# Two attention memories stored with features on partitions, one array of parameters, and the first stage reordered

## The reference

```python
def _rmsnorm(x, g):
    y = xf * lax.rsqrt(jnp.mean(xf * xf, axis=-1, keepdims=True) + EPS)
    return (y * g.astype(jnp.float32)).astype(x.dtype)
...
h = _rmsnorm(x, g_mix[l])
sb_q, ..., xa_q, gate_pre = jnp.split(h @ w_in[l], offsets, axis=-1)
...
# cross attention of the first block: keys and values
k, v = jnp.split(_rmsnorm(mem, g_mem[l]) @ w_mem_kv[l], 2, axis=-1)
# each later layer L: keys and values from the raw second memory
mem_2 @ w_mem_k_2[L],  mem_2 @ w_mem_v_2[L]
```

## Time and profile before

| | |
|---|---|
| median of 3 runs | 1054.83 us (1052.07 to 1055.42) |
| the profiled execution | 1052.53 us, its span 1050.7 us |
| TensorE matmul busy | 1030.6 us, 98% of the span |
| VectorE, ScalarE busy | 730.9 us (70%), 654.1 us (62%) |
| DMA | 167.52 MB, mean 159 GB/s |
| mean granted TensorE clock | 0.997 of full |

### The profile page before, as it was taken

How to read it: one execution, slowest core, us unless ns; L and a number is a source line. 1 busy time by engine, 2 the same in 40 slices (tenths; PEclk the granted TensorE clock), 3 DMA queues, 4 the chain that set the end, 5 groups by cost and what they waited for, 6 DMA issues and landing times.

```text
span 1050.7 us, 19082 instructions
## 1 busy us (share of the span) xinstructions
PE 1030.6 (98%) x8048; PEld 922.0 (88%) x8048; DVE 730.9 (70%) x1085; ACT 654.1 (62%) x924; POOL 13.3 (1%) x18
## 2 busy tenths in 40 slices
PE   6999999999999999999999999999999999999996
PEld 5798987888989999988999998888799999988875
DVE  4684688885747788765565758977884656599686
ACT  6776576564456656544466678657755667776583
POOL 1000000000000000000000000100000000001000
PEclk9999999999999999999999999999999999999999
DMA  8663434666547655566544533422565455344231
GB/s 307 225 202 120 142 124 137 200 200 201 173 149 228 195 179 167 193 223 187 173 160 130 165 125 120 141 83 102 180 199 168 130 161 161 101 143 142 79 116 47
DMA packets 97831, 167.52 MB, mean 159 GB/s; under 512 B 7048, under 2 KB 32530, under 8 KB 97490
## 3 DMA queue, kind: packets, MB, share of 16 engines
q1 hardware_dynamic: 95776, 159.24, 47.3%
q0 software_dynamic: 1472, 5.51, 1.5%
q10 hardware_dynamic: 498, 1.55, 0.4%
HBM read 165.23 MB, written 1.05 MB: 158 GB/s over the span
## 4 chain that ended last, share of the span: by engine, by line
PE 95%; DVE 3%; DMA 1%; ACT 1%; issue 1%; SPq 0%; DVEq 0%
PE proj L598 13%; PE proj L589 13%; PE proj L600 13%; PE proj L599 13%; PE proj L591 13%; PE proj L590 13%; PE mix L935 1%; PE mix L979 1%; PE mix L936 1%; PE mix L634 1%; PE mix L659 1%; PE mix L642 1%; PE mix L968 1%; DVE wlo L1538 1%; DMA raw<-in_w_mem_kv 1%; PE mix L875 1%
## 5 line engine op out<-in xcount | busy, mean ns | idle before, releaser
L1538 DVE TENSOR_TENSOR wlo<-raw,whi 128x1024 fp32r<-128x1024 f32 (+3 forms) x303 | 355.4, 1202 | 139.9 <-ACT whi L1065 138.0
L1065 ACT ACTIVATE whi<-raw 128x1024 fp32r<-128x1024 f32 (+3 forms) x303 | 306.2, 1040 | 148.1 <-PE proj L600 66.5
L589 PE MATMUL proj<-act_hi,whi 128*128 128x256 f32 x1064 | 303.5, 285 | 0.6 <-ACT arena L1082 0.4
L591 PE MATMUL proj<-act_hi,wlo 128*128 128x256 f32 x1064 | 300.9, 283 | 0.0
L590 PE MATMUL proj<-act_lo,whi 128*128 128x256 f32 x1064 | 300.9, 283 | 0.0
L589 PEld LDWEIGHTS proj<-act_hi,whi 128*128 128x128 f32 x1064 | 203.1, 191 | 3.3 <-ACT arena L1082 1.2
L590 PEld LDWEIGHTS proj<-act_lo,whi 128*128 128x128 f32 x1064 | 203.2, 191 | 0.9
L591 PEld LDWEIGHTS proj<-act_hi,wlo 128*128 128x128 f32 x1064 | 203.2, 191 | 0.2
L598 PE MATMUL proj<-whi,y_hi 128*128 128x512 f32 (+1 forms) x340 | 135.1, 397 | 3.8 <-DVE wlo L1538 3.5
L599 PE MATMUL proj<-wlo,y_hi 128*128 128x512 f32 (+1 forms) x340 | 132.4, 389 | 0.0
L600 PE MATMUL proj<-whi,y_lo 128*128 128x512 f32 (+1 forms) x340 | 132.3, 389 | 0.0
(11 more groups left out here) (360 smaller groups left out, 1239.7 us busy)
## 6 DMA issues: line engine op xcount, KB each, us to landing
raw<-in_w_in SPq DMA_DIRECT2D x144, 512.0 KB, 4.4
raw<-in_w_up SPq DMA_DIRECT2D x88, 256.0 KB, 4.2
raw<-in_w_out SPq DMA_DIRECT2D x32, 512.0 KB, 4.3
raw<-in_w_down SPq DMA_DIRECT2D x22, 512.0 KB, 5.4
raw<-in_w_mem_kv SPq DMA_DIRECT2D x8, 512.0 KB, 9.1
raw<-in_w_mem_k SPq DMA_DIRECT2D x8, 512.0 KB, 4.0
raw<-in_w_o SPq DMA_DIRECT2D x8, 512.0 KB, 3.7
raw<-in_w_mem_v SPq DMA_DIRECT2D x8, 512.0 KB, 3.9
```

Source lines behind the costliest of these rows:

```text
L589: mm(o, wh[:, i, wc], hi[:, k0 + i, :], start=begin and j % 2 == 0, stop=False, skip_group_check=True)
L591: last = mm(o, wl[:, i, wc], hi[:, k0 + i, :], start=False, stop=end, skip_group_check=True)
L1065: fn(whi[c % SPLIT][:, 0:w], raw[c % SLOTS][:, 0:w], ACT.Copy).then_inc(s.w_hi, 1)
L1538: tt(wlo[c % SPLIT][:, 0:w], raw[c % SLOTS][:, 0:w], f32(whi[c % SPLIT][:, 0:w]), ALU.subtract).then_inc(s.w_lo, 1)
```

## The change

- Both memories are handed over with features on partitions (`[P, KT, SEQ]`). The first memory's tiles are rounded from SBUF, with no transposes (`mem_upper`, `mem_lower`). SP requests its halves ahead of pieces 0 and 2.
- All parameter rows become one array `params` of 128 x 284 float32, requested by ScalarE in one transfer; the 3 + 11 transposes and the copies of parameters out of PSUM go.
- The sums of squares of the memory now need a sum over partitions: ScalarE squares the whole memory, VectorE adds the eight tiles in one reduction with an inner stride of 256 elements, and TensorE adds over partitions by two matmuls with a column of ones.
- The scaled `x` is turned after half of xav (pieces 4 and 5) rather than before it. `x` is requested ahead of piece 5, not piece 4.
- The rest of the constants is requested after ScalarE has moved xav out; the `tree` table once 16 lower halves are made. The small instructions for lower bounds and rotary angles move behind the softmax of the cross attention, amid sbv.
- The second memory's two turns become one copy on ScalarE and one subtraction on VectorE each.

```diff
-STAGES1, STAGES2 = 8, 5
+STAGES1, STAGES2 = 6, 5
...
+    for name in ("mem", "mem_2"):
+        arrays[name] = np.ascontiguousarray(named[name][0].T.reshape(KT, P, SEQ).transpose(1, 0, 2))
...
-        MEM = ar(4096, NB, DM)
+        MEM, MEM_SQ, MEM_SUM = ar(14336, KT, SEQ), ar(4096, KT, SEQ), ar(8192, SEQ)
...
         def _(sp):
-            sp.dma_start(const[:, 0:P], a["const"][:, 0:P]).then_inc(s.ident_in, 16)
-            for b in range(NB):
-                sp.dma_start(MEM[:, b, :], a["mem"][0, b * P:(b + 1) * P]).then_inc(s.mem_in, 16)
             for c, loads in enumerate(pieces):
-                if c == SLOTS:
+                if c in (0, 2):
+                    half = slice(c * KT // 4, c * KT // 4 + KT // 2)
+                    sp.dma_start(MEM[:, half, :], a["mem"][:, half, :]).then_inc(s.mem_rest if c else s.mem_in, 16)
+                if c == SLOTS + 1:
                     sp.dma_start(X[:, :, :], a["x"][0].rearrange("(b p) d -> p b d", p=P)).then_inc(s.x_in, 16)
...
         def _(pool):
-            pool.wait_ge(s.x_in, 16)
+            pool.wait_ge(s.w_lo, 4 * SLOTS)
             pool.dma_start(TREE_IN[:, :], a["tree"]).then_inc(s.tree_in, 16)
...
# TensorE
+            project("xak", None, MEM_hi, MEM_lo, ready=lambda k: pe.wait_ge(s.mem_lo, k))
+            pe.wait_ge(s.mem_sum, 1)
+            for b in range(NB):
+                last = mm(mix[:, 3, 4 * b:4 * b + 4], MEM_SUM[:, b * P:(b + 1) * P], ONE4, start=True, stop=True)
+            last.then_inc(s.mem_ss, 1)
+            project("xav", None, MEM_hi, MEM_lo, part=(0, 2))
+            pe.wait_ge(s.norm_x, 1)
             pe.wait_ge(s.ident_in, 16)
-            pe.wait_ge(s.gains_in, 16 * 3)
-            for v in range(3):
-                last = nc.tensor.transpose(mix[:, 0, v * 8:(v + 1) * 8], STG8[:, v * P:(v + 1) * P], ident[0:8, 0:8])
-            last.then_inc(s.par_t, 1)
+            turn(KT, lambda k, b: XN[:, b, k * P:(k + 1) * P])
+            project("xav", None, MEM_hi, MEM_lo, part=(2, 4))
             pe.wait_ge(*stage(1, None))
-            pe.wait_ge(s.mem_in, 32)
-            turn(KT, lambda k, b: MEM[:, b, k * P:(k + 1) * P])
-            project("xak", None, MEM_hi, MEM_lo, ready=lambda k: pe.wait_ge(s.mem_lo, k))
...
             project("xaq", None, act_hi, act_lo)
...
-            turn(KT, lambda k, b: MEM2_AT[None][:, b, k * P:(k + 1) * P])
...
-                if L + 1 < LAYERS:
-                    pe.wait_ge(s.mem2_in, 16 * L + 32)
-                    turn(KT, lambda k, b: MEM2_AT[L][:, b, k * P:(k + 1) * P])
                 project("hgf0", L, act_hi, act_lo)
-                if L + 1 < LAYERS:
-                    pe.wait_ge(s.mem2_ok, L + 2)
...
# ScalarE
+            act.dma_start(par[:, :], a["params"]).then_inc(s.params, 16)
+            act.dma_start(const[:, 0:P], a["const"][:, 0:P]).then_inc(s.ident_in, 16)
...
+            mem_upper(range(KT // 2))
             split_until(2)
+            act.wait_ge(s.mem_rest, 16)
+            mem_upper(range(KT // 2, KT))
+            split_until(SLOTS)
+            fn(MEM_SQ, MEM, ACT.Square).then_inc(s.mem_sq, 1)
+            split_until(SLOTS + 1)
+            act.wait_ge(s.x_in, 16)
             for b in range(NB):
-                last = fn(XN[:, b, :], MEM[:, b, :], ACT.Square, accum_out=FIRST_SS[:, b:b + 1])
+                last = fn(XN[:, b, :], X[:, b, :], ACT.Square, accum_out=FIRST_SS[:, b:b + 1])
...
+            split_until(SLOTS + 2)
+            fn(FIRST_R[:, 2:4], FIRST_SS, ACT.Ln, bias=epsb[:, 0:1], scale=1.0 / DM)
+            act.wait_ge(s.mem_ss, 1)
+            link(fn(FIRST_R[:, 0:2], mix[:, 3, 0:8].rearrange("p (b c) -> p b c", c=4)[:, :, 0], ACT.Ln, bias=epsb[:, 0:1], scale=1.0 / DM))
+            fn(FIRST_R, FIRST_R, ACT.Exp, scale=-0.5).then_inc(s.norm_r, 1)
+            split_until(pieces_until("xak", None))
...
             leave_mem("xav", QKV)
+            act.dma_start(const[:, P:], a["const"][:, P:]).then_inc(s.consts, 16)
+            leave("xaq", None, QK[:, 0:8, :].rearrange("p (b h) d -> p b (h d)", b=NB))
...
+            attend_exp(0, XP, XA_D ** -0.5)
+            split_until(ahead_of("sbv", None, 1))
             act.wait_ge(s.tree_in, 16)
             fn(tree[:, :, :, :].rearrange("p b l t -> p (b l t)"), TREE_IN, ACT.Copy).then_inc(s.tree_ok, 1)
             act.wait_ge(s.lb_a, 1)
...
             act.wait_ge(s.trig_in, 1)
-            leave("xaq", None, QK[:, 0:8, :].rearrange("p (b h) d -> p b (h d)", b=NB))
...
             leave("sbv", None, SBV)
             attend_turned(0, XPT)
...
# VectorE
+            mem_lower(range(KT // 2))
+            split_until(2)
+            mem_lower(range(KT // 2, KT))
             split_until(SLOTS)
+            dve.wait_ge(s.mem_sq, 1)
+            nc.vector.tensor_reduce(MEM_SUM, MEM_SQ.rearrange("p k t -> p t k"), AX.X, ALU.add).then_inc(s.mem_sum, 1)
+            split_until(SLOTS + 2)
             norm(0, X, 238)
-            split_until(SLOTS + 1)
+            split_until(SLOTS + 4)
             turned("h", None, KT, act_hi, act_lo, lambda k: cols1[:, 0, k:k + 1]).then_inc(s.mixed, 1)
...
             attend_shares(0, XP, XA_D ** -0.5)
             dve.wait_ge(s.consts, 16)
...
             split_until(pieces_until("sbv", None))
+            dve.wait_ge(s.lb_b, 1)
...
-            turned("mem2", None, KT, MEM_hi, MEM_lo, None).then_inc(s.mem2_ok, 1)
+            dve.wait_ge(s.mem2_hi, 1)
+            tt(MEM_lo, MEM2_AT[None], f32(MEM_hi), ALU.subtract).then_inc(s.mem2_ok, 1)
```

More of the change, by code:

```diff
@@ L85, with by_column, laid_out @@
 PI = 3.1415925
+def by_column(*rows):
+    return np.concatenate([v.reshape(-1, P).T for v in rows], 1)
+PARAM_NAMES = {"block1": ("g_mix", "g_mem", "g_ffn", "ml_conv_w", "ml_conv_b"), "ffn": ("ff_conv_w", "ff_conv_b"),
+               "heads": ("xa_g_q", "xa_g_k", "hgrn_out_norm_2", "mla_q_norm_2", "mla_kv_norm_2"), "logits": ("hgrn_lb_logits_2",)}
+PARAMS = {"block1": 0, "ffn": 8 * KT, "heads": 8 * KT + 8 * FT, "logits": 8 * KT + 8 * FT + 10,
+          "bias": 10 * KT + 8 * FT + 10, "end": 10 * KT + 8 * FT + 18}
+def laid_out(inputs):
+    named = {name: np.asarray(inputs[name]) for name in _INS}
+    arrays = {name: np.ascontiguousarray(named[name]) for name in _WHOLE}
+    bias = np.concatenate([named["ml_b_i"][0], named["ml_b_f"][0]])
+    columns = [by_column(*(named[name] for name in names)) for names in PARAM_NAMES.values()]
+    arrays["params"] = np.ascontiguousarray(np.concatenate([*columns, np.broadcast_to(bias, (P, 2 * ML_H))], 1))
+    for name in ("mem", "mem_2"):
+        arrays[name] = np.ascontiguousarray(named[name][0].T.reshape(KT, P, SEQ).transpose(1, 0, 2))
+    arrays["positions"] = np.ascontiguousarray(named["positions_2"][0].reshape(NB, P).T)
+    arrays["const"], arrays["tree"] = CONST, TREE
+    return arrays
 def piece(w, row, k, col, n):
@@ L198, in __init__ @@
         self.trig_a = new("trig_a")
+        self.mem_rest = new("mem_rest")
+        self.mem_hi = new("mem_hi")
         self.mem_lo = new("mem_lo")
+        self.mem_sq = new("mem_sq")
+        self.mem_sum = new("mem_sum")
+        self.mem_ss = new("mem_ss")
+        self.mem2_hi = new("mem2_hi")
         self.x_lo = new("x_lo")
@@ L1617, in _ @@
             split_until(pieces_until("xav", None))
-            dve.wait_ge(s.par_t, 2)
-            copy(cols1[:, 3:8, :].rearrange("p v k -> p (v k)"), mix[:, 0, 24:64])
-            copy(cols2[:, :, :].rearrange("p v k -> p (v k)"), mix[:, 1, 0:176])
-            copy(cols3[:, :], mix[:, 2, 0:10])
-            copy(lb[:, 0:2, :].rearrange("p v k -> p (v k)"), mix[:, 2, 16:32]).then_inc(s.par_ok, 1)
-            dve.wait_ge(s.par_ok, 1)
+            split_until(pieces_until("xaq", None))
+            for name in ("xak", "xaq"):
+                dve.wait_ge(*out_of(name, None))
+            link(tt(QK_SQ, QK, QK, ALU.mult))
+            nc.vector.tensor_reduce(stat[:, 0:16], QK_SQ, AX.X, ALU.add).then_inc(s.xa_ss, 1)
+            dve.wait_ge(s.xa_r, 1)
+            tt(QK, QK, spread(stat[:, 16:32], P), ALU.mult).then_inc(s.xa_n, 1)
+            split_until(pieces_until("sbq", None))
+            split_until(pieces_until("sbk", None))
+            attend_shares(0, XP, XA_D ** -0.5)
             dve.wait_ge(s.consts, 16)
             LBX, LBL = stat[:, 96:112], stat[:, 112:128]
-            tt(LBX[:, 0:8], lb[:, 0, :], lb[:, 1, :], ALU.subtract)
-            tt(LBX[:, 8:16], lb[:, 1, :], lb[:, 0, :], ALU.subtract).then_inc(s.lb_a, 1)
+            tt(LBX[:, 0:8], logits[:, 0, :], logits[:, 1, :], ALU.subtract)
+            tt(LBX[:, 8:16], logits[:, 1, :], logits[:, 0, :], ALU.subtract).then_inc(s.lb_a, 1)
             nc.vector.memset(cur[:, 4:12], NEG)
@@ L1654, in _ @@
             ts(cos, cos, PI, -PI, ALU.min, ALU.max).then_inc(s.trig_in, 1)
-            dve.wait_ge(s.trig_a, 1)
-            dve.wait_ge(s.tree_ok, 1)
-            split_until(pieces_until("xaq", None))
-            for name in ("xak", "xaq"):
```

(11 more changed lines are left out.)

148 lines of the change are left out of this document (55 added, 93 removed).

## The result

The changed kernel takes 1055.88 us (median of 12 runs, 1053.84 to 1058.73) against 1053.28 us (12 runs, 1051.39 to 1055.42) for the kernel before, measured beside it: a ratio of 1.0029 [1.0020, 1.0038], slightly slower. The forecast was 1046.2 us. The profiled execution of the changed kernel took 1057.93 us, with a span of 1056.1 us, 5.4 us more than before.

The account below looks back on a forecast made before the run. TensorE, busy 98% of the span, was taken as the bound. Second memory -3.5, start -4.7 and sbv +0.7 sum to -7.5 us; from an average of 1053.7 that gives 1046.2 us, range 1042.5 to 1051.

Parts of the forecast that it names:

- Second memory, -3.5: Second memory: two turns of 16 transposes go, each 1.75 us on TensorE's chain, saving 3.5 us.
- this bound: Second memory's saving would be 0 if the time of its turns were cover for something else.
- The start, -4.7: Start up to xaq: piece 0 lands earlier and transposes go, so xaq begins at 35.6 instead of 40.31 us.
- The slow stretch: First matmuls, now in xak: 3.56 us at half clock rate, losing 1.8 us, bounds 0 and twice that.
- Covered steps: Start: other engines keep up; for instance `x` lands near 17 us and its scaling is covered by 1.5 us.
- the first rival: Start gives part back: strided VectorE reduction, at four times 2.29 us, costs 3 to 4 us: 1050 us; chance 0.15.
- The 4 us of cover at `xa_n`: Cross attention's query norms: they end at 57 us and are needed at 61, so no delay.
- sbv: Small instructions moved amid sbv: its move out starts at 86.9 us, delaying the value matmuls; +0.7 us.
- Both middle rivals: Start gives part back (chance 0.15); new wait by the constants or at sbv (chance 0.12); each 1050 us.
- The sum: Whole kernel: second memory -3.5, start -4.7 and sbv +0.7 make -7.5 us.
- counts in full until something else comes late: From xaq to 160 us TensorE is nearly gapless, so whatever brings xaq's 40.31 us forward counts in full.
- The chance for slower: At `xa_n`: piece 16 landing late holds TensorE; slower by 0.3% at 22 us of landing, 1058 at 23; chance 0.03.

Follow-up runs that it names:

- The experiment with wide calls: Changed kernel plus 12 tiny matmul calls and 4 calls of 512 columns on ones in TensorE's idle start: 1044.46 us, ratio 0.9924 to the kernel before.
- 34 calls: Kernel before plus 34 tiny float32 matmul calls (136 instructions) in TensorE's idle start: 1065.25 us, ratio 1.0117.
- 64 calls: 64 tiny matmul calls (256 instructions) in TensorE's idle start: changed kernel 1055.30 us, ratio 1.0027; kernel before 1054.05 us, ratio 0.9997.

## Why the prediction was wrong

**Second memory, -3.5.** Right in kind, 0.5 us too large. The first turn gives 1.75. Of the second, 1.3 remains. Behind uv TensorE now waits for ScalarE, which moves the finished uk out of PSUM (L1349); before, the turn covered that:

```profile
582.91 0.38 PE L617 MATMUL proj<-act_hi,whi 128*128 128x256 f32 x1 [0.27 <-ACT arena L1349]
```

This matmul starts 0.65 us after the one before it, where 0.23 is usual there: 0.4 us are lost. "TensorE has no wait around them" was true and not enough: a turn without a wait around it was cover for a move. The prediction named this bound and put it aside.

**The start, -4.7.** It came to -4.39 by the turn at L718, and xaq began at 35.96 us where 35.6 was forecast:

```profile
35.96 0.39 PE L626 MATMUL proj<-whi,act_hi 128*128 128x512 f32 x1
```

Piece 0 landed at 7.76 us (1.18 + 6.58) where 7.5 was forecast, and the first matmul followed 2.4 us later as taken, at 10.16 rather than 9.9. The slow stretch fell on xak, as said: the matmuls from 10.16 to 13.5 are 0.43 apart, which is half rate, a loss of 1.7 us against 1.8. The experiment with wide calls ahead of it shows the same from the other side. So the step drawn from the Trainium skill ("TensorE: Matmul & The Clock Gate", Part 1), that the throttled state is the default and activity releases it, was right in this trace.

**Covered steps.** The strided reduction was the first rival's core. ScalarE's and VectorE's timelines of the changed kernel:

```profile
15.97 3.93 DVE L1626 TENSOR_REDUCE arena<-arena 128x256 f32<-128x2048 f32 x1 [0.51 <-ACT arena L1158]
```

```profile
47.14 1.06 ACT L1076 ACTIVATE whi<-raw 128x1024 fp32r<-128x1024 f32 x1 [3.78 <-DMA raw<-in_w_in]
...
86.31 1.00 ACT L1087 ACTIVATE arena<-proj 128x1024 f32<-128x1024 f32 x1
```

The reduction took 3.93 us against 2.29 for a contiguous one, 1.7 times as long and not four times, and TensorE did not wait for it. (The contiguous one also leaves 16 sums instead of 256, so the 1.7 is not the stride's alone.) `x` landed in 6.4 us instead of 12.2. ScalarE waited 3.78 us for a piece at 47.14, while the constants (requested at 38.33, 9.2 us to landing) were on their way beside it; that they are the cause is not shown apart. The 4 us of cover at `xa_n` held. sbv was moved out at 86.31 where 86.9 was forecast, and the value matmuls took 3.68 instead of 3.58 us: 0.1 us, not 0.7. Both middle rivals were excluded by the run.

**The sum.** At 594.69 us the changed kernel is 7.30 us ahead; the sum was 7.5. The mechanism and its size were right up to there.

**The step that failed** is the sentence on the start, used for the whole span: "whatever brings 40.31 forward counts in full until something else comes late". Something came late that is no operand: TensorE's own instructions. The prediction counted the removed instructions as time saved and never as a shift of the rest of the stream; it named the issue gaps only as 0.3 us that might go too. The row that speaks of it, issue at L979 with 0.8 us, was in the waits of before. It was too small to draw the eye; the same kernel with 34 calls has 8.5 us there, and a clock penalty. In place of the forecast -7.5 the gain of 7.3 us stood until 595 us and then 11.6 us went: 7.4 in waits for instruction blocks, 4.4 in half clock by the records. The chance for slower was placed on `xa_n` alone.

The Trainium skill has a rule on this ("Runtime: NRT & Kernel Launch", Instruction fetch mechanics): the stream is refilled in blocks of 256 instructions, and crossing a block's end is mostly hidden because instructions are issued more slowly than they are fetched. The block size agrees with the period found here, since 64 calls bring the old time back. That crossings are hidden holds for nearly all of the 63, and fails at these dense groups: 11.8 us between the best-placed and worst-placed form of the kernel before. At the pace of the 146 matmuls above a block lasts about 1.3 us (an estimate, 1.44 us times 256 / 292), and the next one takes 2.2 to 2.7 us from the start of its transfer.

**What is shown and what not.** Shown: position in the instruction stream alone moves either kernel by 8 to 12 us (1047.73 to 1056.09 and 1053.43 to 1065.25); it does so with a period of 256 instructions; the time is lost in gaps at the dense groups and in half clock behind them; the gaps are waits for the next block, by their place and by the transfers' landing in all 31 cases; at equal phase the change is faster. Open: what sets the start of a transfer, and with it why the second group of layer 0 costs 0.5 us in two kernels and 2.0 to 2.3 in three whose block ends lie one or two instructions off; and what sets the half-clock stretch near 185 us that some profiles have.

## What to carry to other kernels

When TensorE is the bound and a group of very short matmuls stands anywhere in the stream, an edit that adds or removes instructions moves the block ends too, and that can cost more than the edit brings. So look for "issue" rows in TensorE's waits in both profiles, and judge an edit of under 1% at several paddings of the stream (here 0, 16, 30 and 48 tiny calls in idle time), before and after at the same phase, with the instruction count read from the trace. The place to look at first is a dense group longer than a block: here the long gaps came only where such a group held two block ends. Once the edit is settled, choose the padding, and make part of it wide matmuls in the idle start so that the first real work runs at full clock.

## What was not expected of the hardware

- Idle-time instructions of a few columns changed the time of the kernel before by a factor of 1.0117 [1.0102, 1.0132], and that of the changed one from 1055.88 to 1048.87 us.
- A dense group of 320 instructions costs nothing or under 1 us where it holds one block end, and 1.76 to 3.40 us in 18 of 23 cases where it holds two.
- A TensorE gap costs up to 2.7 us more behind it: after 9 of the 18 gaps of 1.76 us and more the granted clock is 0.50, for 3.4 or 6.8 us. After the others, as the one at 736.67 (2.25 us), there is no such record.
- The matmuls of the changed kernel run at half rate from 10.2 to 13.6 us, and its first clock record begins at 13.6. A view of an earlier window reads 1.00 only because there is no record.
- A VectorE reduction with an inner stride of 1 KB took 3.93 us, 1.7 times a contiguous one of the same size (which leaves fewer sums).
